# Six modulation chunks from TensorE to VectorE, attention steps from GpSimd to VectorE, fewer loads in the recurrence

## The reference, cut to what matters

```python
# attention, per block of queries
strict = s_idx < t_idx
log_fail = jnp.where(strict, jax.nn.log_sigmoid(-z), 0.0)
after = lax.cumsum(log_fail, axis=3, reverse=True) - log_fail
w = jnp.where(strict, jnp.exp(jax.nn.log_sigmoid(z) + after), 0.0)
# modulation of the second block
mod = jax.nn.silu(c) @ w_ada[layer] + b_ada[layer]
sh1, sc1, g1, sh2, sc2, g2 = jnp.split(mod, 6, axis=-1)
```

## Time and profile before

| | us |
|---|---|
| three runs | 1134.72, 1134.81, 1140.17 |
| median | 1134.81 |
| the profiled execution's own time | 1133.99 |
| its span | 1132.1 |
| mean granted clock of TensorE in it | 0.991 |

### The profile page before, as it was taken

The page is one execution under the profiler, slowest core; times in us unless marked ns, Lnnn a source line. Parts: engine busy times, 40 slices in busy tenths (PEclk is TensorE's granted clock), DMA queues, the critical chain, the costliest instruction groups (busy, mean ns, idle before and its releaser), DMA issues.

```text
span 1132.1 us, 17911 instructions
## 1 busy us (share of the span) xinstructions
PE 1058.2 (93%) x7545; PEld 720.2 (64%) x7545; DVE 461.8 (41%) x698; ACT 354.1 (31%) x508; POOL 39.5 (3%) x32
## 2 busy tenths in 40 slices
PE   5999999999999999999999999999899989898986
PEld 4997877799789999877986453444244433242432
DVE  4784244367655353557648351222122212121212
ACT  4752322364454343455543220111011111010102
POOL 0001310001000101000000000000000000000000
PEclk9999999999999999999989999999999999999999
DMA  9444377434545655463465869999999999999994
GB/s 318 147 174 159 135 236 238 139 145 173 187 130 183 190 186 186 186 219 130 167 224 209 363 257 421 419 419 421 420 421 421 420 421 421 421 420 421 420 420 191
DMA packets 95445, 316.31 MB, mean 279 GB/s; under 512 B 8262, under 2 KB 33174, under 8 KB 70678
## 3 DMA queue, kind: packets, MB, share of 16 engines
q1 hardware_dynamic: 94342, 312.70, 72.1%
q10 hardware_dynamic: 1040, 2.69, 0.7%
HBM read 314.32 MB, written 1.05 MB: 279 GB/s over the span
## 4 chain that ended last, share of the span: by engine, by line
PE 72%; DMA 21%; DVE 4%; ACT 2%; issue 1%; SPq 0%; POOL 0%; DVEq 0%; ACTq 0%
DMA arena<-in_w 20%; PE bank L1474 11%; PE bank L767 11%; PE bank L769 11%; PE bank L768 11%; PE bank L1498 4%; PE bank L753 4%; PE bank L1018 3%; PE bank L933 2%; PE bank L1454 1%; PE bank L967 1%; PE bank L744 1%; PE bank L1511 1%; PE bank L714 1%; DVE arena L2560 1%
## 5 line engine op out<-in xcount | busy, mean ns | idle before, releaser
L1474 PE MATMUL bank<-ring,hT 128*64 128x512 f32 x512 | 227.0, 595 | 29.8 <-DMA arena<-in_w 28.6
L1474 PE MATMUL bank<-arena,hT 128*64 128x512 f32 x512 | 227.0, 595 | 0.0
L769 PE MATMUL bank<-h_high,ring_low 128*128 128x256 f32 x688 | 193.8, 282 | 0.0
L1474 PEld LDWEIGHTS bank<-ring,hT 128*64 128x64 f32 x512 | 67.8, 137 | 182.2 <-issue 130.2
L558 DVE TENSOR_TENSOR ring_low<-ring,hi_high 128x2048 fp32r<-128x2048 f32 (+2 forms) x58 | 126.0, 2218 | 100.8 <-ACT hi_high L1645 100.8
L767 PE MATMUL bank<-h_high,hi_high 128*128 128x256 f32 x528 | 148.1, 280 | 0.0
L768 PE MATMUL bank<-h_low,hi_high 128*128 128x256 f32 x528 | 147.5, 279 | 0.0
L1645 ACT ACTIVATE hi_high<-ring 128x2048 fp32r<-128x2048 f32 (+2 forms) x58 | 104.5, 1854 | 92.0 <-DMA ring<-in_w_ffn_up 33.9
L769 PEld LDWEIGHTS bank<-h_high,ring_low 128*128 128x128 f32 x688 | 130.8, 190 | 0.0
L1498 PE MATMUL bank<-arena 128*64 128x512 f32 x384 | 113.3, 595 | 7.1 <-DVE hT L2772 6.7
L2778 DVE TENSOR_TENSOR arena<-arena,bank 128x512 f32<-128x512 f32 x16 | 17.4, 1084 | 231.0 <-ACT arena L2002 231.0
(11 more groups left out here) (401 smaller groups left out, 1706.7 us busy)
## 6 DMA issues: line engine op xcount, KB each, us to landing
arena<-in_w SPq DMA_DIRECT2D x112, 1024.0 KB, 23.0
ring<-in_w SPq DMA_DIRECT2D x80, 1024.0 KB, 20.5
ring<-in_w_in SPq DMA_DIRECT2D x12, 2048.0 KB, 7.8
ring<-in_w_ada SPq DMA_DIRECT2D x7, 2048.0 KB, 8.2
ring<-in_w_ffn_gate SPq DMA_DIRECT2D x11, 1024.0 KB, 5.5
ring<-in_w_ffn_up SPq DMA_DIRECT2D x11, 1024.0 KB, 8.2
ring<-in_w_ada SPq DMA_DIRECT2D x20, 512.0 KB, 5.0
ring<-in_w_ffn_down SPq DMA_DIRECT2D x5, 2048.0 KB, 7.9
```

What stands on the lines that cost most here:

```text
L769: return mm(ps, a[1], b[0], start=False, stop=stop)
L1474: last = mm(both(6 + half, x), hg[:, k, (2 * q + x) * CAP:(2 * q + x + 1) * CAP], w13s[x][k // 4][:, k % 4, half * EF:(half + 1) * EF], st ...
```

## The change

1. Chunks 0 to 5 are multiplied on VectorE (`ada_products`): one `tensor_scalar` and seven `scalar_tensor_tensor` steps of 128 x 512, from the ring slot and with silu(c) as scalar of each partition, each waiting for the one before. TensorE only sums the result over partitions, now against ones. Their copies on ScalarE go. Chunk 0 to 3 lie beside attention, 4 and 5 in the recurrence's levels, a quarter of chunk 4 in each of levels 1 to 4.
2. GpSimd's sums and masks of attention, and its copy `cb`, go to VectorE.
3. Bank order: sums 0 to 2 stand between the heads' tiles, sum 3 in the outputs; chunks 10 and 11 are still multiplied on TensorE, after `u` and after `phi` 2, and summed after `m`.
4. Ring: gate chunk 0 keeps slot 1; chunks 0 to 5 alternate between slots 2 and 0, freed when VectorE has used them. In quarters are only chunk 11, gate 1 and gate 2.
5. Mixing: tile 1's transposes come before tile 0's second output tile.

```diff
@@ plan_banks
-    for mm in range(2):
-        o += [("ga", mm)] + [("l", h) for h in range(4 * mm, 4 * mm + 4)]
+    o += [("ga", 0), ("l", 0), ("l", 1), ("as", 0), ("l", 2), ("l", 3)]
+    o += [("ga", 1), ("as", 1), ("l", 4), ("l", 5), ("as", 2), ("l", 6), ("l", 7)]
     o += [("tok", 1, a) for a in range(4)]
-    o += [("o", 0), ("o", 1)] + ada_banks(0) + [("o", 2), ("o", 3)]
+    o += [("o", 0), ("o", 1), ("as", 3), ("o", 2), ("o", 3)]
...
@@ sync
-            stream(("ada", c), [(0, cols(A["w_ada_2"][0], c * 512, c * 512 + 512))], ("ad", c))
+            used = ("sem", "ada_acc", ADA_DVE.index(c) + 1) if c in ADA_DVE else ("ad", c)
+            stream(("ada", c), [(0, cols(A["w_ada_2"][0], c * 512, c * 512 + 512))], used)
...
+        def slot_of(n):
+            if n <= held:
+                return n % RING
+            if n <= held + 6:
+                return (held + 1 + (n - held - 1) % 2) % RING
+            return (n - 1) % RING
+        last_level = LEVELS - 1
+        PACED = {("ada", 11): (("dt", 0, last_level - 1, 1), ("dt", 1, last_level - 1, 1), ("x", 1, last_level, 0)),
+                 ("gate", 1): (("w1", 1, 0), ("u", 0, 0), ("u", 1, 0)),
+                 ("gate", 2): (("phi", 1), ("ry", 1, 0), ("phi", 2))}
@@ tensor
                     if h % 4 == 2:
                         last.then_inc(*full(("ga", j)))
+                    if h:
+                        ada_sum(h // 2 - 1)
                     pe.wait_ge(S("att_sp"), j + 1)
                     two = [write(pe, ("l", h + e)) for e in range(2)]
...
                 if p == 2:
-                    ada(0)
+                    ada_sum(3)
...
-            ada(1)
...
-                ada(lv + 1)
+                if lv == LEVELS - 1:
+                    ada_sum(4)
...
-            ada(LEVELS + 1)
...
-            ada(LEVELS + 2)
+            ada_chunk(10)
+            ada_sum(5)
...
             phi_of(2)
+            ada_chunk(11)
             y_inside(0)
...
+            ada_sum(10)
+            ada_sum(11)
             for j in range(2, 5):
                 gates_of(j)
...
+            mix_transposes(0)
+            ada_sum(8)
+            drained(pe, ("pm",))
+            mixed_out(0, 0)
+            mix_transposes(1)
+            mixed_out(0, 1)
+            ada_chunk(9)
+            mixed_out(1, 0)
+            ada_sum(9)
+            mixed_out(1, 1)
@@ vector
+            def one_minus(half):
+                dve.wait_ge(S("att_ln"), half + 1)
+                hs = slice(4 * half, 4 * half + 4)
+                link(V.tensor_tensor(rz[:, hs, :], rz[:, hs, :], az[:, hs, :], ALU.add))
+                V.tensor_tensor(diagonal(rz, half), diagonal(rz, half), strict, ALU.mult).then_inc(S("att_sp"), 1)
+            def weights(half):
+                dve.wait_ge(S("att_x"), half + 1)
+                V.tensor_tensor(diagonal(az, half), diagonal(az, half), strict, ALU.mult).then_inc(S("att_w"), 1)
+            def ada_products(c, k0, k1):
+                w, acc = slot_view(("ada", c), KD), modp[c]
+                if k0 == 0:
+                    arrived(dve, ("ada", c))
+                    dve.wait_ge(S("csil"), 1)
+                for k in range(k0, k1):
+                    if k == 0:
+                        ins = V.tensor_scalar(acc, w[:, k, :], csil[:, k:k + 1], None, ALU.mult)
+                    else:
+                        ins = V.scalar_tensor_tensor(acc, w[:, k, :], csil[:, k:k + 1], acc, ALU.mult, ALU.add)
+                    if k < KD - 1:
+                        link(ins)
+                    else:
+                        ins.then_inc(S("ada_acc"), 1)
             for i in range(NT):
                 ps = filled(dve, ("v", i))
                 V.tensor_copy(vtok[:, i, :], ps[:, :]).then_inc(*free(("v", i)))
+                if i == 0:
+                    ada_products(0, 0, 5)
+                one_minus(i)
...
+            ada_products(0, 5, KD)
+            to_tokens(0)
+            ada_products(1, 0, KD)
+            later_weights(0)
+            ada_sum(0)
+            ada_products(2, 0, KD)
+            later_weights(2)
+            ada_sum(1)
+            ada_products(3, 0, 4)
+            weights(0)
+            later_weights(4)
+            ada_products(3, 4, KD)
+            ada_sum(2)
+            later_weights(6)
+            to_tokens(1)
+            weights(1)
+            ada_sum(3)
+            V.tensor_scalar(cb, cast(csil.unsqueeze(2), P, KD, 32), 1.0 / 32, None, ALU.mult).then_inc(S("cb"), 1)
...
             for lv in range(1, LEVELS):
-                ada_sum(ADA_EARLY[lv])
+                if lv < LEVELS - 1:
+                    ada_products(4, 2 * lv - 2, 2 * lv)
+                else:
+                    ada_sum(4)
+                    ada_products(5, 0, 2)
...
-            ada_sum(ADA_EARLY[LEVELS])
-            ada_sum(ADA_EARLY[LEVELS + 1])
+            ada_products(5, 2, KD)
+            ada_sum(5)
```

More of the change, by code:

```diff
@@ L217, in plan_banks @@
     o += [("yd", 1, a) for a in range(2)] + [("yo", a) for a in range(2)] + [("as", 7), ("ad", 8)]
[L218 to L221, removed]
+    o += [("mt", 0, a) for a in range(2)] + [("as", 8), ("mx", 0, 0)] + [("mt", 1, a) for a in range(2)]
+    o += [("mx", 0, 1), ("ad", 9), ("mx", 1, 0), ("as", 9), ("mx", 1, 1)]
     o += [("x5", 0, c) for c in range(4)] + [("rt",)] + [("x5", 1, c) for c in range(4)] + [("rk",)]
@@ L505, in build @@
         SLOTS, loads = {}, [0] * RING
[L507 to L515, removed]
+        held = [key for key, _, _ in W].index(("gate", 0))
+        def slot_of(n):
[8 more added lines that the diff above has]
+                 ("gate", 2): (("phi", 1), ("ry", 1, 0), ("phi", 2))}
         for n, (key, parts, last) in enumerate(W):
-            loads[n % RING] += 16 * (4 if key in PACED else len(parts))
-            SLOTS[key] = (n % RING, loads[n % RING])
+            loads[slot_of(n)] += 16 * (4 if key in PACED else len(parts))
+            SLOTS[key] = (slot_of(n), loads[slot_of(n)])
         def slot_view(key, k):
@@ L906, in ada_sum @@
                     for k in range(KD):
[L907 removed]
+                        last = mm(ps[o:o + 64, k:k + 1], modp[c][:, 64 * k:64 * k + 64], K("ones")[:, 0:1],
                                   start=True, stop=True)
@@ L1373, in _, with mix_transposes @@
             ada_chunk(8)
-            for i in range(NT):
+            def mix_transposes(i):
                 pe.wait_ge(S("ys"), i + 1)
@@ L2295, in to_tokens @@
                 V.tensor_copy(vp[:, i, :, :], ps[:, :].rearrange("p (h d) -> p h d", h=HEADS)).then_inc(*free(("tok", i, 3)))
-            to_tokens(0)
-            for h in range(HEADS):
-                ps = filled(dve, ("l", h))
-                V.tensor_scalar(az[:, h, :], ps[:, 0:384], 0.0, None, ALU.min).then_inc(*free(("l", h)))
-            to_tokens(1)
-            def heads4(ps):
-                return ps[:, :].rearrange("p (h t) -> p h t", h=4)
-            def four(ps):
-                return ps[:, 0:4 * CH].rearrange("p (h t) -> p h t", h=4)
             def ada_sum(c):
@@ L2319, in ada_sum, with later_weights, heads4, four @@
                     V.tensor_tensor(g, g, ps[:, :], ALU.add).then_inc(*free(("as", c)))
+            def later_weights(h):
+                for e in range(2):
+                    ps = filled(dve, ("l", h + e))
+                    V.tensor_scalar(az[:, h + e, :], ps[:, 0:384], 0.0, None, ALU.min).then_inc(*free(("l", h + e)))
+            ada_products(0, 5, KD)
[16 more added lines that the diff above has]
+            V.tensor_scalar(cb, cast(csil.unsqueeze(2), P, KD, 32), 1.0 / 32, None, ALU.mult).then_inc(S("cb"), 1)
             dve.wait_ge(S("gate_in"), 48)
+            def heads4(ps):
+                return ps[:, :].rearrange("p (h t) -> p h t", h=4)
+            def four(ps):
+                return ps[:, 0:4 * CH].rearrange("p (h t) -> p h t", h=4)
             dve.wait_ge(S("pc"), 1)
```

80 lines of the change are left out of this document (28 added, 52 removed).

## The result

The changed kernel takes **1143.2 us** in the median (1140.1 to 1143.8, five runs), the kernel before 1135.1 (five runs). The ratio is 1.0054, with a 95% interval from 1.0029 to 1.0079: slower by about half a per cent, outside the range of 1126 to 1140. The profiled execution, the shortest of the five, took 1140.06 with a span of 1137.9, 5.8 us more than the span before. Measured again beside the kernel before on another chip, the ratio was 1.0057 (1.0034 to 1.0079).

The account below looks back on a forecast made before the run. TensorE, busy for 93% of the span, was taken as the bound. Attention +11.6, recurrence -17.2 and +4.1 after it sum to -1.5, from 1133.99 to 1132.5; 0.8 more for the median gives 1133.3 us, range 1126 to 1140.

Parts of the forecast that it names:

- Attention: Stage before the grams: product 0 out, sums 0 to 3 in, waits and a clock loss added; +11.6 us in all.
- the wait: In attention, TensorE stands 7.9 us before head 4's scores, until ScalarE's sigmoids of gate tile 0 free the bank.
- Recurrence: From the grams to the first ry: products and sums leave TensorE, taking 61.8 us to 44.6; -17.2 us.
- The +1.5 for the lost cover: Recurrence, level 1: VectorE's masks and copies, covered by product 1 before, delay the last x tile to 9.4 us; +1.5.
- most of the weight loads there are gone, so I take half: -0.8: Recurrence: half of TensorE's 1.6 us idle time, in levels under load traffic, goes; -0.8 us, bounds 0 and 1.6.
- the price of what was moved: Recurrence: seven products (13.3 us) and eight sums (8.7) go out; sum 4, product 10 and sum 5 (4.1) come back.
- After it: Between phi and the gates, after the recurrence: product 11 (1.9) and sums 10 and 11 (2.2) on TensorE; +4.1 us.
- Gate chunks 1 to 3 are loaded later [...] Hidden; cost if not, the difference.: After the recurrence: chunk 1 there by 207, chunk 3 by 215, wanted at 219 and some 222; no cost forecast.
- the removed work was cover: Rival in the recurrence: without 0.5 us margin a level, each of five levels loses about 1; 1138.3 us, chance 0.15.
- From the gates on: Gates to the end: mixing transposes, ScalarE's copies and constants each cost 0, and the earlier shift is carried on.
- The clock rival: Rival: clock falls in the recurrence's five levels, 29 us of 64-column matmuls, half at lower level; 1147.8 us, chance 0.12.
- VectorE is quicker: Rival in attention: VectorE's steps beat their rows; 1123.7 us without the wait, 1128.5 with steps at 0.5; chance 0.23.

Follow-up runs that it names:

- the 32 records more: Changed kernel with sum 1 computed five times over, 32 matmul records more on TensorE before head 4's scores; ratio 1.0022 (1.0006 to 1.0038).
- the version of 1128.3: Changed kernel plus five edits: gate-tile-0 sigmoids earlier, minimums before chunk products, gate chunks 2 and 3 held, sum 2 earlier, router loads later; 1128.3 us, ratio 0.9916.

## Why the prediction was wrong, point by point

**Attention: right** (+11.6 forecast, +11.5 measured). A scalar_tensor_tensor step with its link takes 5.48 / 7 = 0.78 us; heads 2 and 3 are done at 133.3, as forecast; TensorE stood 8.4 us for 7.9; grams at 156.5 for 156. Small errors cancel in it: a sum took some 0.9 us and not 1.05, the wait was 0.5 us and the clock 0.3 us dearer. VectorE and ScalarE of the changed kernel:

```profile
119.27 5.47 DVE L2299 SCALAR_TENSOR_TENSOR arena<-ring,small,arena 128x512 f32<-128x512 f32 x7
...
126.92 5.48 DVE L2299 SCALAR_TENSOR_TENSOR arena<-ring,small,arena 128x512 f32<-128x512 f32 x7
132.31 1.01 DVE L2333 TENSOR_SCALAR arena<-bank 128x384 f32<-128x384 f32 x2
...
137.64 0.49 DVE L2297 TENSOR_SCALAR arena<-ring,small 128x512 f32<-128x512 f32 x1 [4.24 <-DMA ring<-in_w_ada]
```

```profile
133.43 1.28 ACT L1750 ACT_TABLE_LOAD   x1 [21.08 <-DVE arena L2333]
134.72 1.48 ACT L1750 ACTIVATE arena<-arena 128x1536 f32<-128x1536 f32 x1
136.22 1.28 ACT L1738 ACT_TABLE_LOAD   x1
137.52 0.84 ACT L1738 ACTIVATE arena<-bank,parcol 128x256 f32<-128x256 f32 x2
```

This is the chain that the earlier trace rows had in small: last minimum, exponential, sigmoid, bank. The clock cost 2 us there, for 1.7: from 138.4 to 142.4 TensorE worked at 0.51. Chunk 3 came at 137.6, not 135.7, and VectorE waited 4.2 us for it, not 2; as forecast, it held up nobody else.

**Recurrence: mechanism right, two terms off** (-17.2 forecast, -15.8 measured). The +1.5 for the lost cover came true: TensorE waits for VectorE's masks (0.39 and 0.51 us) and copies, and the last x tile of level 1 is through some 9.5 us after the start of the grams, for 9.4. One step that was off is "most of the weight loads there are gone, so I take half: -0.8". The other pauses came to 1.3 us (0.22, 0.40, 0.64) where 1.6 had been before: -0.3. I halved them with the loads, without asking what they were. The other is the price of what was moved. The grouped lines add up busy times, which overlap at the edges; from start to start a product takes 1.86 us (149.64 to 151.50 before), a column sum 0.98, a row sum 1.05. So 21.1 us went out and 4.0 came in, 17.2 in all and not 17.9. These two make 1.2 of the 1.4.

**After it: this step failed** (+4.1 forecast, +9.2 measured). "Gate chunks 1 to 3 are loaded later [...] Hidden; cost if not, the difference." The data were in time, and the gates waited for nothing. I had asked only whether the one who uses the load gets it in time, and not who else uses the DMA engines meanwhile. Pauses cost 2.7 us more than before (3.86 - 1.12) and the fall of the clock behind them 2.2 (1.8 in L1146, 0.4 in the last y records), some 5 in all. The rival "the removed work was cover" named loads of the gates in a burst beside short matmuls; it put them into the levels at 1 us each and came to 1138.3 with a chance of 0.15. Its place and its price were wrong, and among what could be late it didn't have TensorE's own code.

**From the gates on: no term** (0 forecast, +1.0 measured). The clock fell once more at 261.8, 1.5 us. The kernel before falls at 315.7 instead, for about 0.6 us of what is lost here. Eleven of the fourteen traces have a fall that starts between 250 and 268 us; the kernel before, the 32 records more and the version of 1128.3 don't, and these three have one between 309 and 317 instead. Why is open.

**The clock rival** said that the clock falls in the recurrence. There it stayed at 1.00. It fell in the y stage, which the text of that rival didn't look at, and behind pauses. "VectorE is quicker" fell: the steps run at 0.75.

Sum of what was missed: 1.4 + 5.1 + 1.0 = 7.5 on a forecast of -1.5 is +6.0, with a span 5.8 us longer. The medians lie 8.2 apart, mainly since the profiled execution is the shortest of its five. The three longer ones (1143.2 to 1143.8) had a mean granted clock of 0.981 to 0.982 instead of 0.984, which points to further falls of the clock; no trace of them shows where.

## What to carry to other kernels

A load that is hidden from its user can still delay the code of an engine. Where TensorE runs several hundred short matmuls, look at pauses ended by "issue", count the matmuls between them, look for instruction packets in the DMA queues, and keep 2 MB loads out of that stretch, as far as their users allow. When VectorE gets long work, put every short step that another engine waits for ahead of the next long one; here that alone was worth 6.9 us in attention, of which 4 to 5 were left at the end (the ratio is 1.0013, the changed kernel's 1.0054 and 1.0057).

## What the runs showed of the hardware that I had not expected

- TensorE stops at ends of 16 KB blocks of code, 0.2 to 3.7 us, and goes on 1.2 to 1.6 us after the instruction packet has landed. The pauses of all kernels here stand at the same record numbers from the program's start, near 125 apart, whatever the work at that place. With no loads in flight, three blocks of 64-column matmuls passed with no pause over 0.2 us; with a DMA share near 1, single pauses reached 3.7 us.
- Thirty-two matmul records more, some 75 us earlier, moved a pause by 32 records.
- A scalar_tensor_tensor with two inputs in SBUF and a GpSimd tensor_tensor hold each other up: 7.3 us for three steps instead of 2.3.
- In or right behind pauses of TensorE of 2.1 to 4.0 us the clock fell to its lower level in every trace that has one (once for 17 us), but for one pause of 2.89 us in the recurrence.
